# Mixture-of-experts rows: one gather per chunk by a list made with one-hot products, in place of a scatter into expert order

## The chip, the cores and the metric

One Trainium2 chip, one core. The metric is the device time of one launch in microseconds, as the median of several runs; the kernel before has 1685.17 us (three runs, 1684.55 to 1685.78). All data is float32.

## The reference

Two transformer-like blocks run one after the other on 512 tokens of width 1024. The last part of the second is a mixture of experts with 16 experts of hidden width 512; every token uses two of them. The change touches only this part and what prepares it:

```python
def hier_moe(x, w_group, b_group, w_expert, b_expert, w_gate, w_up, w_down):
    t = x.reshape(-1, D)                                   # 512 tokens x 1024
    pg = softmax(t @ w_group + b_group)                    # 4 groups
    gsel, pg_sel = argmax(pg), max(pg)
    e_logits = (t @ w_expert + b_expert).reshape(-1, 4, 4)[token, gsel]
    top_p, top_i = top_k(softmax(e_logits), 2)             # 2 experts of the group
    gates = one_hot(gsel * 4 + top_i, 16) * pg_sel * top_p / sum(top_p), summed over the 2
    y = 0
    for e in range(16):
        h = silu(t @ w_gate[e]) * (t @ w_up[e])
        y = y + gates[:, e:e + 1] * (h @ w_down[e])
    return y
```

`t` is the normalised residual; the output is `rms_norm(h + y) * final_norm`. Before this stand a state-space mixer, cross-attention, a convolutional feed-forward block, and a second pair of mixers with an output product (`w_out_2`).

## The kernel before, in words

Every engine has one instruction stream written by hand, in the order of the functions in `pe_program`, `act_program`, `dve_program`, `pool_program` and `sp_program`. Engines meet only through counting semaphores. Float32 products are made as three products: each operand is split into a high part (ScalarE copies it to the 32-bit "r" type, `w_hi`, `xh`, `hh`) and a low part (VectorE subtracts, `w_lo`, `xl`, `hl`), and TensorE adds hi·hi, hi·lo and lo·hi (L410 to L412 in the dense parts, L2810 to L2812 in the experts). SyncE queues the weight loads, 1 MB each.

**Output product** (`pe_w_out2`, L2342). Eight blocks of 128 features. After each one `pe_w_out2_turn` (L2326) makes the router logits of all tokens, as 20 rows by 512 columns (L2332, one float32 product per block, weights `wr`, added up over the blocks in bank 4), and turns the block into token rows with four transposes. ScalarE copies these to `xtm` (L2371) and sums their squares (L2373); VectorE scales them by the gain into `htm` (L2399).

**Routing** (`dve_route`, L2500). VectorE copies the logits out of PSUM, TensorE turns them back to token rows, VectorE scales and biases them per token tile (L2516, four instructions), and finds group and experts by small comparisons. `pre` holds running sums over the four token tiles (L2540). Two products, with a matrix of ones and a strictly triangular one, give each token's rank inside its experts and the count of each expert (L2459, L2460). From these VectorE builds `pick` (L2559), with which TensorE finds the token in each row of expert 0 (L2463), and writes this list to `first` (L2574). Then come `slot_of` (the row of each of a token's two copies in expert order, L2588) and `table` (which experts have more than 128 rows and need further chunks, L2600). Rows in expert order lie in chunks of 128, chunk e belonging to expert e; overflow chunks come after chunk 15.

**Moving the rows.** SyncE stores the normalised rows to DRAM, `scratch_rows` (L2738). GpSimd gathers chunk 0 from there by the list `first` (L2441, into `wrow`, also called `x_first`), and then scatters all rows, two copies of each, into `slot_rows` in DRAM with eight indirect transfers (L2446). When all eight have landed, SyncE loads chunk 1 and chunk 2 (`sp_rows`, L2713, called at L2741 and L2743) between two weight loads, and each later chunk once TensorE has turned the chunk two before it (L2752). `slot_rows` and eight chunks of `result_rows` are filled with zeros much earlier, in `pool_zero` (L2312), by 24 and 8 transfers of 512 KB.

**Experts** (`pe_experts`, L2816, with `act_experts`, `dve_experts`, `sp_experts`, `pool_experts`). A chunk has six weight parts of 1 MB: two of gate, two of up, two of down. Part n of chunk c is loaded when the low part of the same n of chunk c-1 is made. TensorE turns the rows ("x", eight transposes, L553), multiplies parts 0 to 3 (12 products each), turns the hidden rows ("h", four transposes), and multiplies parts 4 and 5. The orders are lists (`pe_order`, `act_order`, `dve_order`), and waits are counts in them. In steady state TensorE's order is w0 of c+1, h of c, w1 of c+1, x of c+2, w4 and w5 of c, w2 and w3 of c+1. Chunks 0 to 14 are written out. In the first, the order is x(0), w0, w1, x(1), w2, w3. On VectorE the low parts 2 to 5 of chunk 0 and the gates stand in `dve_route` (L2602), ahead of the rows of chunk 0 (L3004). A loop then runs chunk 15 and any overflow chunk (with this data the loop runs once); in each turn it also fetches the rows and weights of one further chunk, whether they are needed or not, and TensorE turns those rows (L2874) before the hidden rows of the turn. Results go to `result_rows` from GpSimd (L2772).

**End.** GpSimd gathers each token's two results by `slot_of` (L3059), and VectorE and ScalarE combine and normalise them.

## Time and profile before

| what | value |
|---|---|
| median of the runs | 1685.17 us |
| the profiled execution: its own time | 1681.13 us |
| its span, first to last instruction | 1680.0 us |
| TensorE busy / VectorE / ScalarE / GpSimd | 88% / 62% / 45% / 8% of the span |
| mean granted TensorE clock | 0.942 of full speed |
| DMA, mean over the span | 148 GB/s, 248.34 MB |
| the chain that ended last, by engine | TensorE 76%, VectorE 14%, ScalarE 5%, issue 2%, DMA 1%, GpSimd 1% |

Times are in us from the start of the span. In the trace the output product runs from about 1270 to 1318, routing until 1334, the chunks 0 to 14 until 1633, the loop turn until 1647, the end until 1680. A line of a timeline gives the start, the duration, the engine, the line of the kernel, the operation, output<-input with shapes, the number of merged instructions, and in brackets the idle time before it and what ended it. Matmuls are pipelined, so the distance of two starts says more than the duration.

### The profile page before, as it was taken

To read this page: it belongs to the slowest core of one execution; us is meant where nothing else is said; L and a number is where in the kernel's file an instruction comes from. 1 tells how busy PE (TensorE), PEld (TensorE's weight loads), DVE (VectorE), ACT (ScalarE), POOL (GpSimd) and SP (SyncE) were. 2 spreads that over 40 slices of the span, in tenths; PEclk is the share of its full clock that TensorE was granted. 3 is DMA by queue.
4 is the path that set the end of the run, shared out by engine and by line. 5 is a ranking of instruction groups with operands and counts; after the bars stand their busy time and mean duration, and the time that the engine had idled before them with its cause. 6 is when DMAs were issued, how large, how long until landed. Compare 5 with 4: busy or idle time off the path is not lost.

```text
span 1680.0 us, 17325 instructions
## 1 busy us (share of the span) xinstructions
PE 1485.0 (88%) x6792; PEld 1150.5 (68%) x6792; DVE 1039.4 (62%) x1342; ACT 756.8 (45%) x994; POOL 137.7 (8%) x162
## 2 busy tenths in 40 slices
PE   3889948979978999999999999999988499999981
PEld 1667618758756788788878778786545378888871
DVE  5849976465333555445554648845444668888876
ACT  4453315554333422122223443244445568878763
POOL 5400000000003100000000113200000200000002
PEclk8899869989999999999999999999999799999996
DMA  5121214212213922232212221110003599999984
GB/s 193 63 75 51 75 30 146 76 51 75 76 50 120 396 85 85 77 127 100 82 63 94 101 101 51 68 59 26 25 1 127 210 390 404 412 412 409 415 337 175
DMA packets 45953, 248.34 MB, mean 148 GB/s; under 512 B 6960, under 2 KB 8240, under 8 KB 23728
## 3 DMA queue, kind: packets, MB, share of 16 engines
q1 hardware_dynamic: 31488, 207.14, 32.3%
q0 software_dynamic: 9888, 36.18, 5.7%
q10 hardware_dynamic: 4496, 3.91, 0.7%
q8 instruction: 54, 0.88, 0.2%
q14 instruction: 27, 0.22, 0.0%
HBM read 213.66 MB, written 33.55 MB: 147 GB/s over the span
## 4 chain that ended last, share of the span: by engine, by line
PE 76%; DVE 14%; ACT 5%; issue 2%; DMA 1%; POOL 1%; ACTq 1%; DVEq 0%; POOLq 0%
PE bank L410 14%; PE bank L411 14%; PE bank L412 14%; PE bank L2810 5%; PE bank L2812 5%; PE bank L2811 5%; PE bank L553 3%; DVE w_lo L366 1%; PE bank L429 1%; PE bank L2133 1%; PE bank L2162 1%; DVE bu L832 1%; PE bank L430 1%; PE bank L431 1%; PE bank L469 1%
## 5 line engine op out<-in xcount | busy, mean ns | idle before, releaser
L410 PE MATMUL bank<-h_hi,w_hi 128*128 128x512 f32 x952 | 392.8, 413 | 28.8 <-DVE h_lo L490 19.6
L411 PE MATMUL bank<-h_lo,w_hi 128*128 128x512 f32 x952 | 381.8, 401 | 0.0
L412 PE MATMUL bank<-h_hi,w_lo 128*128 128x512 f32 x952 | 381.5, 401 | 0.0
L366 DVE TENSOR_TENSOR w_lo<-w_raw,w_hi 128x2048 fp32r<-128x2048 f32 (+3 forms) x89 | 197.5, 2219 | 91.6 <-ACT w_hi L360 90.9
L410 PEld LDWEIGHTS bank<-h_hi,w_hi 128*128 128x128 f32 x952 | 183.1, 192 | 86.9 <-DVE h_lo L490 20.6
L412 PEld LDWEIGHTS bank<-h_hi,w_lo 128*128 128x128 f32 x952 | 183.4, 193 | 43.1
L411 PEld LDWEIGHTS bank<-h_lo,w_hi 128*128 128x128 f32 x952 | 183.5, 193 | 40.8 <-issue 1.9
L360 ACT ACTIVATE w_hi<-w_raw 128x2048 fp32r<-128x2048 f32 (+3 forms) x89 | 158.4, 1780 | 59.9 <-PE bank L412 59.9
L2991 DVE TENSOR_TENSOR h_lo<-w_raw,h_hi 128x2048 fp32r<-128x2048 f32 x32 | 73.3, 2292 | 18.1 <-ACT h_hi L2893 18.1
L2991 DVE TENSOR_TENSOR lo_b<-raw_b,hi_b 128x2048 fp32r<-128x2048 f32 x32 | 73.2, 2288 | 14.2 <-ACT hi_b L2893 14.2
L410 PE MATMUL bank<-a_hi,w_hi 128*128 128x512 f32 x176 | 69.4, 395 | 4.5 <-DVE a_lo L1574 4.5
L411 PE MATMUL bank<-a_lo,w_hi 128*128 128x512 f32 x176 | 69.7, 396 | 0.0
L412 PE MATMUL bank<-a_hi,w_lo 128*128 128x512 f32 x176 | 69.1, 393 | 0.0
L1538 ACT ACTIVATE gc<-gc 128x512 f32<-128x512 f32 x22 | 13.9, 634 | 118.6 <-DVE gc L899 118.6
L2893 ACT ACTIVATE hi_b<-raw_b 128x2048 fp32r<-128x2048 f32 x32 | 61.1, 1911 | 10.1 <-PE bank L2812 10.1
L2893 ACT ACTIVATE h_hi<-w_raw 128x2048 fp32r<-128x2048 f32 x32 | 61.0, 1909 | 0.0
L2810 PE MATMUL bank<-h_hi,hh 128*128 128x512 f32 x128 | 53.0, 414 | 5.8 <-DVE hl L3015 4.4
L2810 PE MATMUL bank<-hi_b,xh 128*128 128x512 f32 x128 | 52.3, 409 | 6.3 <-DVE xl L3002 6.3
L1572 DVE TENSOR_TENSOR gc<-gc,bank 128x512 f32<-128x512 f32 x22 | 15.2, 689 | 61.9 <-PE bank L412 61.9
L2811 PE MATMUL bank<-h_hi,hl 128*128 128x512 f32 x128 | 51.6, 403 | 0.0
L2812 PE MATMUL bank<-h_lo,hh 128*128 128x512 f32 x128 | 51.4, 401 | 0.0
L2812 PE MATMUL bank<-lo_b,xh 128*128 128x512 f32 x128 | 50.7, 396 | 0.0
(556 smaller groups left out, 2817.0 us busy)
## 6 DMA issues: line engine op xcount, KB each, us to landing
w_raw<-in_params_dram SPq DMA_DIRECT2D x122, 1024.0 KB, 5.1
raw_b<-in_params_dram SPq DMA_DIRECT2D x51, 1024.0 KB, 7.9
slot_rows<-prm POOLq DMA_DIRECT2D x24, 512.0 KB, 19.4
w_raw<-in_params_dram SPq DMA_DIRECT2D x16, 704.0 KB, 4.0
xg<-slot_rows SPq DMA_DIRECT2D x16, 512.0 KB, 8.1
result_rows<-osb POOLq DMA_DIRECT2D x16, 512.0 KB, 8.1
result_rows<-prm POOLq DMA_DIRECT2D x8, 512.0 KB, 36.5
xt<-in_x_t_dram POOLq DMA_DIRECT2D x1, 2048.0 KB, 9.5
```

The source lines that it names most:

```text
L360: A.activation(k.w_hi[:, g % SPLIT, 0:size], k.raw[:, g % RAW, 0:size], ACT.Copy).then_inc(s.w_hi, 1)
L366: V.tensor_tensor(k.w_lo[:, g % SPLIT, 0:size], k.raw[:, g % RAW, 0:size], k.w_hi[:, g % SPLIT, 0:size].bitcast(F32), ALU.subtract).then_i ...
L410: PE.matmul(ps, wh, hi[:, c, 0:width], start=c == 0, stop=False)
L411: PE.matmul(ps, wh, lo[:, c, 0:width], start=False, stop=False)
L412: m = PE.matmul(ps, wl, hi[:, c, 0:width], start=False, stop=c == parts - 1)
L429: PE.matmul(ps, xh, wh, start=c == 0, stop=False)
L553: return k.nc.tensor.transpose(out, in_, k.ident[0:n, 0:n])
L2810: PE.matmul(o, xh[:, k0 + c, :], wh, start=first and c == 0, stop=False)
L2811: PE.matmul(o, xl[:, k0 + c, :], wh, start=False, stop=False)
L2812: m = PE.matmul(o, xh[:, k0 + c, :], wl, start=False, stop=final and c == 3)
L2893: done(A.activation(w_hi[n], raws[n], ACT.Copy), "w", n, c)
L2991: done(V.tensor_tensor(w_lo[n], raws[n], w_hi[n].bitcast(F32), ALU.subtract), "w", n, c)
```

## The change

The scatter, `slot_rows` and its 24 zero fills go away, and the eight fills of `result_rows` are spread out behind product blocks of the feed-forward part. VectorE makes, for all 16 chunks at once, the two factors of a one-hot product (`at_row`: which row of its chunk a token's copy takes, 128 columns; `tok_in`: the token's number in the column of its chunk), and eight products on TensorE give `tok`, the list of tokens of every chunk. GpSimd gathers each chunk from `scratch_rows` by a column of `tok`. What needs the overflow chunks (`slot_of`, `table`, the lists of chunks 16 to 23, the gates) moves out of the routing into the last written-out chunk: `dve_route_over` on VectorE, after the hidden rows of chunk 14, and `pe_tokens(k, 5, 0, OVER + 1)` on TensorE, before parts 4 and 5 of chunk 14. The router logits are made in token rows directly, four products of 20 columns per block. TensorE's first chunk becomes x(0), w0, w1, w2, w3, x(1), and on VectorE the rows of chunk 0 come before its low parts 4 and 5.

```diff
     k.g(G.memset(k.zero, 0.0))
     k.g.own()
-    rows, results = (x.rearrange("(n p) (u c) -> n p u c", p=P, u=2) for x in (k.slot_rows, k.result_rows))
+    results = k.result_rows.rearrange("(n p) (u c) -> n p u c", p=P, u=2)
     source = k.zero.rearrange("p (o c) -> p o c", o=1).broadcast_to([P, 2, T])
-    for n in range(SLOT_TILES):
-        G.dma_start(rows[n], source).then_inc(s.zeroed, 16)
     for n in range(E, SLOT_TILES):
+        G.wait_ge(s.gemm, BLOCK0["up0"] + 2 * (n - E))
         G.dma_start(results[n], source).then_inc(s.zeroed, 16)
...
         PE.wait_ge(s.mo_in, 1)
-    m = PE.matmul(k.bank[4][0:20, :], k.wr[:, b, :], k.xt[:, b, :], start=b == 0, stop=b == DB - 1)
+    for t in range(TT):
+        m = PE.matmul(k.bank[4][:, t * 20:t * 20 + 20], k.xt[:, b, t * P:t * P + P], k.wr[:, b, :], start=b + t == 0,
+                      stop=b == DB - 1 and t == TT - 1, skip_group_check=True)
     if b == DB - 1:
...
         A.wait_ge(s.mo_sq, b)
-    a(A.activation(k.xtm[:, :, b * P:b * P + P], turned(k, b), ACT.Copy))
+    if b < DB - 1:
+        act_w_out2_copy(k, b)
...
+def pool_rows(k, ids, i):
+    k.nc.gpsimd.indirect_dma_start(out=k.xg[:, i, :], out_offset=None, in_=k.dram["rows"][:, :],
+                                   in_offset=bass.IndirectOffsetOnAxis(ap=ids, axis=0)).then_inc(k.s.x_load1 if i else k.s.x_load0, 16)
...
     G.iota(k.tokid[:, :], [[P, TT]], base=0, channel_multiplier=1).then_inc(s.mo_iota, 1)
-    G.wait_ge(s.zeroed, ZEROED)
+    G.wait_ge(s.row_stored, 16 * TT)
     G.wait_ge(s.mo_slot, 1)
-    G.wait_ge(s.row_stored, 16 * TT)
-    G.indirect_dma_start(out=k.x_first[:, :], out_offset=None, in_=k.dram["rows"][:, :],
-                         in_offset=bass.IndirectOffsetOnAxis(ap=k.first[:, 0:1], axis=0)).then_inc(s.x_first, 16)
-    G.wait_ge(s.mo_slot, 2)
-    for t in range(TT):
-        for i in range(2):
-            G.indirect_dma_start(out=k.slot_rows[:, :], out_offset=bass.IndirectOffsetOnAxis(ap=k.slot_of[:, i, t:t + 1], axis=0),
-                                 in_=k.htm[:, t, :], in_offset=None).then_inc(s.scattered, 16)
+    for c in range(2):
+        pool_rows(k, k.tok[:, c:c + 1], c)
...
+def pe_tokens(k, ins, buffer, columns):
+    for i in range(2):
+        k.nc.tensor.wait_ge(k.s.mo_in, ins + i)
+        for t in range(TT):
+            m = k.nc.tensor.matmul(k.bank[7][:, 0:columns], k.at_row[buffer][:, i, t, :], k.tok_in[buffer][:, i, t, 0:columns],
+                                   start=i + t == 0, stop=i + t == TT)
+    m.then_inc(k.s.mo_cnt, 1)
 def pe_route(k):
...
-    for t in range(TT):
-        m = pe_turn(k, k.bank[7][:, t * 20:t * 20 + 20], k.lgs[:, t * P:t * P + P])
-    m.then_inc(s.mo_lgt, 1)
     PE.wait_ge(s.mo_htm, DB)
+    PE.wait_ge(s.mo_row, 1)
     PE.wait_ge(s.mo_in, 2)
     counts = k.bank[HBANK][:, 0:(TT + 1) * E]
-    PE.matmul(counts, k.ones[:, :], k.pre[:, :, :].rearrange("p t e -> p (t e)"), start=True, stop=False)
-    PE.matmul(counts[:, 0:TT * E], k.stri[:, :], k.r16[:, 0, :, :].rearrange("p t e -> p (t e)"), start=False, stop=True).then_inc(s.mo_cnt, 1)
-    PE.wait_ge(s.mo_in, 3)
+    PE.matmul(counts[:, 0:TT * E], k.stri_r, k.sel.rearrange("p t e -> p (t e)"), start=True, stop=False, skip_group_check=True)
     for t in range(TT):
-        m = PE.matmul(k.bank[7][:, 0:1], k.pick[:, t, :], k.tok_f[:, t:t + 1], start=t == 0, stop=t == TT - 1)
+        later = k.sel[:, t, :].rearrange("p (o e) -> p o e", o=1).broadcast_to([P, TT - t, E])
+        m = PE.matmul(counts[:, (t + 1) * E:].rearrange("p (n e) -> p n e", e=E), k.ones_r, later, start=False, stop=t == TT - 1,
+                      skip_group_check=True)
     m.then_inc(s.mo_cnt, 1)
+    pe_tokens(k, 3, 1, E)
 def act_route(k):
...
+def dve_at_row(k, buffer, row):
+    V, s = k.nc.vector, k.s
+    place = k.place.rearrange("p (o c) -> p o c", o=1).broadcast_to([P, TT, P])
+    for i in range(2):
+        at = row[:, i, :].rearrange("p (t o) -> p t o", o=1).broadcast_to([P, TT, P])
+        V.tensor_tensor(k.at_row[buffer][:, i, :, :], place, at, ALU.is_equal).then_inc(s.mo_in, 1)
...
-    V.wait_ge(s.zeroed, ZEROED)
-    V.wait_ge(s.mo_lgt, 1)
-    V.tensor_copy(k.lgs, k.bank[4][0:20, :]).then_inc(s.mo_lg, 1)
...
-        v(V.scalar_tensor_tensor(k.L[:, t, :], k.bank[7][:, t * 20:t * 20 + 20], rstd[:, t:t + 1], k.row[:, slice(*ROWS["router_b"])], ALU.mult, ALU.add))
+    V.wait_ge(s.mo_lgt, 1)
+    v(V.tensor_tensor(k.L[:, :, :], k.bank[4][:, 0:TT * 20].rearrange("p (t c) -> p t c", t=TT),
+                      rstd.rearrange("p (t o) -> p t o", o=1).broadcast_to([P, TT, 20]), ALU.mult))
+    v.own()
+    v(V.tensor_tensor(k.L[:, :, :], k.L[:, :, :], k.rows("router_b", TT, 20), ALU.add))
...
-        v.own()
-        x = V.tensor_tensor(k.pre[:, t + 1, :], k.pre[:, t, :], k.r16[:, 0, t, :], ALU.add)
-        if t == TT - 1:
-            x.then_inc(s.mo_in, 1)
-        else:
-            v(x)
+    V.tensor_tensor(k.sel.rearrange("p t (g j) -> p t g j", g=4), ohg4, wide(both), ALU.mult).then_inc(s.mo_in, 1)
     for i, oh in ((1, oh1), (2, oh2)):
         v(V.tensor_tensor(v16(i), ohg4, wide(oh), ALU.mult))
+    v.own()
+    pair = k.r16[:, 1:3, :, :]
+    for i in range(2):
+        v(V.tensor_tensor(k.tok_in[1][:, i, :, :], pair[:, i, :, :], k.tok_f[:, :].rearrange("p (t o) -> p t o", o=1).broadcast_to([P, TT, E]), ALU.mult))
     f = lambda x: x.rearrange("p t o -> p (t o)")
     v(V.tensor_tensor(e2, f(m2), f(m1), ALU.subtract))
     V.tensor_tensor(ex, gl, gm.broadcast_to([P, TT, 4]), ALU.subtract).then_inc(s.mo_dve, 1)
...
+    V.wait_ge(s.mo_cnt, 1)
+    mine = k.r16[:, 3:5, :, :]
+    rank = k.bank[HBANK][:, 0:TT * E].rearrange("p (o x) -> p o x", o=1).broadcast_to([P, 2, TT * E])
+    v(V.tensor_tensor(mine.rearrange("p i t e -> p i (t e)"), pair.rearrange("p i t e -> p i (t e)"), rank, ALU.mult))
+    v.own()
+    v(V.tensor_reduce(k.rk[:, 0, :, :].rearrange("p i (t o) -> p (i t) o", o=1), mine.rearrange("p i t e -> p (i t) e"), AX.X, ALU.add))
+    v.own()
+    dve_at_row(k, 1, k.rk[:, 0, :, :])
+    v(V.tensor_copy(k.ranks, k.bank[HBANK][:, 0:(TT + 1) * E]))
+    V.wait_ge(s.mo_cnt, 2)
+    V.tensor_copy(k.tok[:, 0:E], k.bank[7][:, 0:E]).then_inc(s.mo_slot, 1)
+    for n in (2, 3):
+        dve_expert_lo(k, k.dve_event, 0, n)
+    dve_expert_rows(k, 0)
+    for n in (4, 5):
+        dve_expert_lo(k, k.dve_event, 0, n)
+def dve_route_over(k):
+    V, s, v = k.nc.vector, k.s, k.v
     tiles, ends, base, delta, one = (k.cnt[:, i, :] for i in range(5))
+    rank = k.ranks[:, 0:TT * E].rearrange("p (t e) -> p t e", t=TT)
+    n_e = k.ranks[:, TT * E:]
     rows = lambda x: x.rearrange("p (o e) -> p o e", o=1).broadcast_to([P, TT, E])
-    V.wait_ge(s.mo_cnt, 1)
-    rank = k.bank[HBANK][:, 0:TT * E].rearrange("p (t e) -> p t e", t=TT)
-    n_e = k.bank[HBANK][:, TT * E:TT * E + E]
-    v(V.tensor_tensor(k.r16[:, 3, :, :], rank, rows(k.eoff[:, 0, :]), ALU.add))
-    v.own()
-    for t in range(TT):
-        x = V.tensor_scalar(k.pick[:, t, :], k.place[:, :], k.r16[:, 3, t, 0:1], k.r16[:, 0, t, 0:1], ALU.is_equal, ALU.mult)
-        if t == TT - 1:
-            x.then_inc(s.mo_in, 1)
-        else:
-            v(x)
     v(V.tensor_scalar(tiles, n_e, float(P), None, ALU.is_gt))
     for j in range(2, TT):
         v.own()
...
-    V.wait_ge(s.mo_cnt, 2)
-    V.tensor_copy(k.first[:, :], k.bank[7][:, 0:1]).then_inc(s.mo_slot, 1)
     v(V.scalar_tensor_tensor(delta, base, float(P), k.eoff[:, 1, :], ALU.mult, ALU.add))
...
-    v(V.tensor_reduce(slots, pair.rearrange("p i t e -> p (i t) e"), AX.X, ALU.add))
-    v.own()
...
+    rk, past, row, slot = (k.rk[:, i, :, :] for i in range(4))
+    v(V.tensor_reduce(slot.rearrange("p i (t o) -> p (i t) o", o=1), pair.rearrange("p i t e -> p (i t) e"), AX.X, ALU.add))
+    v.own()
+    V.tensor_copy(k.slot_of[:, :, :], slot).then_inc(s.mo_slot, 1)
...
+    v(V.tensor_scalar(past, rk, float(P), None, ALU.is_ge))
+    for j in range(2, TT):
+        v.own()
+        v(V.scalar_tensor_tensor(past, rk, float(P * j), past, ALU.is_ge, ALU.add))
+    v.own()
+    v(V.scalar_tensor_tensor(row, past, float(-P), rk, ALU.mult, ALU.add))
+    v.own()
+    v(V.tensor_tensor(slot, slot, row, ALU.subtract))
+    v.own()
     n = OVER + 1
+    for i in range(2):
+        tile = slot[:, i, :].rearrange("p (t o) -> p t o", o=1).broadcast_to([P, TT, n])
+        v(V.tensor_tensor(k.tok_in[0][:, i, :, 0:n], k.over[:, :].rearrange("p (o q) -> p o q", o=1).broadcast_to([P, TT, n]), tile, ALU.is_equal))
+    v.own()
+    for i in range(2):
+        token = k.tok_f[:, :].rearrange("p (t o) -> p t o", o=1).broadcast_to([P, TT, n])
+        v(V.tensor_tensor(k.tok_in[0][:, i, :, 0:n], k.tok_in[0][:, i, :, 0:n].bitcast(F32), token, ALU.mult))
+    v.own()
+    dve_at_row(k, 0, row)
...
-    for n in range(2, 6):
-        dve_expert_lo(k, k.dve_event, 0, n)
...
+    V.wait_ge(s.mo_cnt, 3)
+    V.tensor_copy(k.tok[:, E:], k.bank[7][:, 0:n]).then_inc(s.mo_slot, 1)
...
-    part(1, 2)
-    SP.wait_ge(s.scattered, 16 * 2 * TT)
-    sp_rows(k, 1, 1)
-    part(1, 3)
-    sp_rows(k, 2, 0)
+    for n in range(2, 6):
+        part(1, n)
     for n in (0, 1):
         part(2, n)
...
         if c + 2 < FIXED:
-            SP.wait_ge(s.m_pe, PE_AT["x", 1, c + 1])
-            sp_rows(k, c + 3, (c + 3) % 2)
...
-        SP.wait_ge(s.m_pe, q * len(PE_LOOP) + PE_BEFORE["x", 1])
-        sp_rows(k, q + E, LOOP_BUFFER)
...
 def pool_experts(k):
     G, s = k.nc.gpsimd, k.s
+    def rows(c):
+        G.wait_ge(s.m_pe, PE_AT["x", 1, c - 2])
+        pool_rows(k, k.tok[:, c:c + 1], c % 2)
+    rows(2)
+    rows(3)
     for c in range(FIXED):
+        if c + 4 < E:
+            rows(c + 4)
         G.wait_ge(s.m_act, ACT_AT["o", 1, c])
         pool_result(k, c, c % 2)
+    G.wait_ge(s.mo_table, 1)
...
+        G.wait_ge(s.m_pe, q * len(PE_LOOP) + PE_BEFORE["x", 1])
+        G.wait_ge(s.m_dve, q * len(DVE_LOOP) + (len(DVE_AT) + DVE_LOOP["i", 0]))
+        G.tensor_tensor(k.act_scrap[:, 1:2], k.ones[:, 0:1], k.ones[:, 0:1], ALU.add).then_inc(s.pool_step, 1)
+        pool_rows(k, k.tok_next[:, 0:1], LOOP_BUFFER)
+        G.wait_ge(s.pool_step, q + (k.g.n + 1))
         G.wait_ge(s.m_act, q * len(ACT_LOOP) + (len(ACT_AT) + ACT_LOOP["o", 1]))
         pool_result(k, q + FIXED, LOOP_BUFFER)
...
-        if c == 0:
-            PE.wait_ge(s.x_first, 16)
-        else:
-            PE.wait_ge(s.x_load1 if c % 2 else s.x_load0, 16 * ((c + 1) // 2))
+        PE.wait_ge(s.x_load1 if c % 2 else s.x_load0, 16 * (c // 2 + 1))
+        if c:
             PE.wait_ge(s.m_dve, DVE_AT["x", 1, c - 1])
         for half in range(2):
-            done(pe_turn_x(k, k.xg[:, c % 2] if c else k.x_first, half), "x", half, c)
+            done(pe_turn_x(k, k.xg[:, c % 2], half), "x", half, c)
...
-    PE.wait_ge(s.mo_slot, 1)
     rows(0)
     part(0, 0)
-    part(0, 1)
+    for n in range(1, 4):
+        part(0, n)
     rows(1)
-    part(0, 2)
-    part(0, 3)
...
             rows(c + 2)
+        else:
+            pe_tokens(k, 5, 0, OVER + 1)
         part(c, 4)
         part(c, 5)
         if c + 1 < FIXED:
...
+    act_expert_hi(k, done, 1, 2)
     rows(1)
-    act_expert_hi(k, done, 1, 2)
...
+    dve_expert_lo(k, done, 1, 0)
+    dve_expert_lo(k, done, 1, 1)
+    hidden(0)
+    dve_expert_rows(k, 1)
+    for c in range(FIXED):
+        if c:
+            hidden(c)
         dve_expert_lo(k, done, c + 1, 2)
         dve_expert_lo(k, done, c + 1, 3)
...
+        else:
+            dve_route_over(k)
         dve_expert_lo(k, done, c + 1, 4)
...
+        V.tensor_copy(k.tok_next[:, :], k.tok[:, bass.ds(q + E, 1)]).then_inc(s.m_dve, 1)
```

## Rows read from the trace of the kernel before

**Rows 1.** Busy time by window: from:to, length, PE, PEld, DVE, ACT, POOL, PEclk, DMA share, GB/s.

```profile
540.00:560.00 20.00, 20.00 (x84) 16.38 (x84) 11.62 (x14) 8.59 (x10) 12.50 (x18) 0.94 1.01 389
...
1400.00:1440.00 40.00, 40.00 (x190) 32.97 (x189) 36.15 (x23) 31.85 (x27) 1.06 (x2) 1.00 1.01 414
```

**Rows 2.** The chain in order of time around the routing: start, us, what.

```profile
1318.18 0.60 ACT xtm L2371
...
1346.55 5.22 DMA slot_rows<-htm,slot_of
1351.78 3.23 DMA xg<-slot_rows
```

**Rows 3.** GpSimd's timeline, 1295 to 1375.

```profile
1332.48 1.07 POOL L2441 DMA_INDIRECT wrow<-scratch_rows,first  x1 [61.53 <-DVE first L2574]
...
1335.16 1.96 POOL L2446 DMA_INDIRECT slot_rows<-htm,slot_of  x1 [0.30 <-issue]
...
1344.01 0.96 POOL L2446 DMA_INDIRECT slot_rows<-htm,slot_of  x1 [0.30 <-issue]
```

**Rows 4.** VectorE's timeline, 1300 to 1375.

```profile
1320.94 0.68 DVE L2516 SCALAR_TENSOR_TENSOR L<-bank,rt,row 128x20 f32<-128x20 f32 x4
...
1325.99 0.80 DVE L2540 TENSOR_TENSOR pre<-pre,r 128x16 f32<-128x16 f32 x4
...
1331.47 0.16 DVE L2574 CAST first<-bank 128x1 int32<-128x1 f32 x1 [1.09 <-PE bank L2463]
...
1333.98 2.28 DVE L2991 TENSOR_TENSOR w_lo<-raw_b,w_hi 128x2048 fp32r<-128x2048 f32 x1
...
1343.61 1.28 DVE L3002 TENSOR_TENSOR xl<-bank,xh 128x512 fp32r<-128x512 f32 x2
```

**Rows 5.** TensorE's timeline, 1300 to 1367.

```profile
1305.03 1.03 PE L2332 MATMUL bank<-xt,w_router 128*20 128x512 f32 x2
1305.99 0.66 PE L553 MATMUL bank<-ident,xt 128*128 128x128 f32 x4
...
1329.50 1.87 PE L2463 MATMUL bank<-tok_f,sqs 128*128 128x1 f32 x8 [1.47 <-DVE sqs L2559]
1336.80 1.94 PE L553 MATMUL bank<-ident,wrow 128*128 128x128 f32 x8 [5.43 <-DMA wrow<-scratch_rows,first]
1345.04 0.77 PE L2810 MATMUL bank<-hi_b,xh 128*128 128x512 f32 x1 [6.30 <-DVE xl L3002]
...
1351.77 0.39 PE L2812 MATMUL bank<-lo_b,xh 128*128 128x512 f32 x1
...
1362.94 0.40 PE L2810 MATMUL bank<-hi_b,xh 128*128 128x512 f32 x1
...
1365.70 0.60 PE L553 MATMUL bank<-ident,hid 128*128 128x128 f32 x4
```

**Rows 6.** Line L1728, small float32 products: ns min/median/max, first and last start.

```profile
L1728 PE MATMUL bank<-lf,ones x12: 256/256/256, 1009.1 to 1010.8; 128*128 128x8 f32 x12
...
L1728 PE MATMUL bank<-lf,tri x8: 170/256/256, 1009.0 to 1011.0; 128*128 128x8 f32 x8
```

**Rows 7.** TensorE's timeline, last written-out chunk and loop.

```profile
1614.45 0.66 PE L553 MATMUL bank<-ident,hid 128*128 128x128 f32 x4 [0.85 <-DVE hid L3011]
1619.50 0.77 PE L2810 MATMUL bank<-h_hi,hh 128*128 128x512 f32 x1 [4.39 <-DVE hl L3015]
...
1638.41 1.03 PE L553 MATMUL bank<-ident,xg 128*128 128x128 f32 x8
1639.35 0.66 PE L553 MATMUL bank<-ident,hid 128*128 128x128 f32 x4
```

**Rows 8.** VectorE's timeline, the same stretch.

```profile
1618.72 0.68 DVE L3015 TENSOR_TENSOR hl<-bank,hh 128x512 fp32r<-128x512 f32 x1
...
1630.08 2.29 DVE L2991 TENSOR_TENSOR h_lo<-w_raw,h_hi 128x2048 fp32r<-128x2048 f32 x1 [0.52 <-ACT h_hi L2893]
```

**Rows 9.** The page's DMA issues: KB each, median us to landing.

```profile
result_rows<-osb POOLq DMA_DIRECT2D x16, 512.0 KB, 8.1
```

86 lines of the change are left out of this document (44 added, 42 removed).

## The prediction

> **What bounds the kernel now.** I read the windows first, then the chain in order of time, then each engine's timeline at the places where TensorE stands still. In the expert stage the windows show TensorE busy for all of the 40 us at full clock, with the DMA engines busy all the time too, at 414 GB/s, and VectorE idle for under 4 us [rows 1]. A chunk takes 17.8 us: the hidden rows of chunk 0 are turned at 1365.70, those of chunk 14 at 1614.45, and (1614.45 - 1365.70)/14 = 17.8 [rows 5, 7]. The data is moved for about 7.3 MB a chunk (6 weight parts of 1.05, rows 0.52, result 0.52), which is 410 GB/s. TensorE sets the pace, with the DMA engines close behind. So the change can gain only where TensorE waits: between the end of the output product and about 1363, and at 1614 to 1619. The chain through the first stretch runs over VectorE's routing, GpSimd's issue of the scatter, its landing (5.22 us) and the load of chunk 1 (3.23 us) [rows 2]. TensorE's own timeline shows two waits there: 6.30 us for `xl` before the first product at 1345.04, and the turning of chunk 1 only at 1355.05. At the far end it waits 4.39 us for `hl` [rows 7].
>
> **Zero fills: 0.** The 24 removed fills saturate the DMA engines at 540 to 560, while TensorE is busy for all of the 20 us [rows 1]: the loads run three slots ahead and cover them. Gain 0, at most 1 us. GpSimd's eight remaining waits hold up nothing; it has no work there.
>
> **Logits: -0.6.** Before, a block's logits cost the distance from L2332 to the transposes, 1305.99 - 1305.03 = 0.96 us [rows 5]. After, they are four float32 products, two passes each. L1728's twenty passes with 8 columns start from 1009.0 to 1011.0, 2.0/19 = 0.11 apart [rows 6]. 8 x 0.11 = 0.88. Eight blocks: 8 x 0.08 = -0.6. Upper bound: the transposes' whole duration, 0.66/4 = 0.165 [rows 5], makes 1.3 a block, +2.9; lower bound: 0.94/8 = 0.12 is already what transposes of 128 columns are apart [rows 7], so nothing below -0.6 is expected. I take 0.11, since L1728 is the same kind of product at full clock.
>
> **List of tokens ready: -1.6.** Off the path to it: ScalarE's last copy to `xtm` (0.60, 0.5 between starts) [rows 2], half of L2516's 0.68 (four small instructions become two), and L2540's 0.80 (the running sums go into TensorE's products) [rows 4]: 0.5 + 0.3 + 0.8 = 1.6. The copy comes back ahead of the row scaling, where it fills the time it left. The rank products become five instead of two float32 ones; the list itself needs two 128-element steps (0.6), two 512-element comparisons (1.28, as L3002) and four closing products of 0.235 (L2463: 1.87 for 8 passes [rows 5]), 3.2 against 3.5 before. I call both level together. `first` was written at 1331.63 [rows 4]; the new list stands at 1330.0.
>
> **First rows: -5.6.** GpSimd starts the gather 0.85 later (1331.63 to 1332.48) and it arrived 4.3 after that (1332.48 to 1336.80) [rows 3, 5]: 1335.15. But VectorE now makes low parts 2 and 3 just then. Beside these subtractions an indirect issue took 1.96, and 0.96 once they were over [rows 3]; I add 0.9: 1336.0. The Trainium skill, "GPSIMD Engine Reference", section 1 Specifications, says that GpSimd shares its SBUF interfaces with VectorE and contends with its instructions that have two SBUF inputs; the trace agrees, and without that 0.9 the rows would come at 1335.1. Transposes (1.94), ScalarE's 0.6, VectorE's 0.68 and handovers of 0.2 make 3.4: the first product starts at 1339.4, against 1345.04. VectorE is free by then, 1330.0 + 2 x 2.2 = 1334.4, since parts 4 and 5 and the gates come later; before, they held `xl` back to 1343.61 [rows 4]. 5.6 us.
>
> **First chunk: -2.9.** From first product to first hidden turn it took 1365.70 - 1345.04 = 20.7, with the wait for the scatter inside. After: parts 0 and 1 as before, 7.0 (1351.77 + 0.23 - 1345.04), parts 2 and 3 at 2.76 (1362.94 to 1365.70 is one) = 5.5, the transposes of chunk 1 at full clock 0.94 (1638.41 to 1639.35 [rows 7]), then a new exposed handover, because x(1) now stands directly before w0 of chunk 1: 1.6 (0.6 + 0.68 + latencies; VectorE comes to it late, after a low part and the hidden rows), and 2.76. Sum 17.8, so -2.9. SyncE's queue loses the waits for scatter and rows; the weights of chunk 1 are there by about 1350, and part 4 is wanted after 1363. Together hidden(0) comes 8.5 earlier, 1357.2 against 1365.7, and the 0.6 of the logits besides.
>
> **Steady chunks: 0.** Gathers are issued 15 us before TensorE needs them; the bytes and the 4 KB row pieces are the same. That room of 15 us is the cover. VectorE's subtraction took 2.28 beside the scatter and 2.29 far from it [rows 4, 8], so it isn't slowed.
>
> **Overflow routing: +6.5.** It stands on VectorE after `hl` of chunk 14 (1618.72 + 0.6), and TensorE's `pe_tokens` waits for it with parts 4 and 5 queued behind. 21 instructions of 4 to 128 elements at 0.2 (L2540: 0.80 for four) are 4.3, two of 512 elements 1.3: 5.6. TensorE then closes four products at 0.235, plus 0.1. Part 4 starts at 1626.0 where it started at 1619.50 [rows 7, 8]. Nothing hides it: TensorE has no other work, and ScalarE, SyncE and the loop wait for part 4. The slow start of the products after a wait (half clock) is there in both. The rest of `dve_route_over` (2 us) ends before the next low part can be made, in 1634.
>
> **Rows of the loop: +0.3.** TensorE turns the next chunk's rows in the loop, at 1638.41 [rows 7], or 1644.9 after the 6.5. Before, they were loaded at 1615. Now GpSimd may issue only when VectorE has entered the loop, after the last low part: 1630.08 + 2.3 + 6.5 = 1638.9 [rows 8]. A handover (0.85), its small instruction (0.5) and 4.3 to 5.2 for the gather: 1644.6 to 1645.4. I take 0.3; if it lands after 8.1 us, as results do in this stage [rows 9], 3.4.
>
> **Sum:** -0.6 - 5.6 - 2.9 + 6.5 + 0.3 = -2.3 us (the -1.6 is in the -5.6). Against the profiled execution: 1681.13 - 2.3 = 1678.8. That execution was 4.0 below the median of 1685.17; I apply the difference to the median: 1682.9. About 0.2%, 3.4 us, is what a measurement of this kernel can tell from no change.
>
> **Rivals.**
> (a) The start gains more, -5. The first gather isn't slowed (lands 1335.1), and the clock, at half for seven products from 1345.04 (0.43 instead of 0.23), is up already because the wait ahead is 1.5 instead of 6.3 us: -0.9 - 1.4 = -4.6. For: the shorter wait. Against: TensorE has stood still 5 us before the transposes. 1680.3.
> (b) The loop's rows come late: +3.1 over the forecast, and 1.4 more if the clock falls: +0.8 to +2.2, 1686.0 to 1687.4. For: loads in this stage take 8.1 us. Against: few transfers are queued then.
> (c) The gather holds VectorE. Place: each steady chunk. `hl` is ready 0.8 us before TensorE needs it; if an issue of 1.9 us blocks VectorE there, TensorE loses 1.1 x 13 = 14 us: 1697. It decides from 0.8 us of blocking at that spot. For this, the Trainium skill, "SBUF — State Buffer", has a rule that the shared pair of ports is an exclusive lock, the second comer waiting for a whole instruction. Against: subtraction at 2.28 beside the scatter. This is the case slower than before.
> (d) The change doesn't do what it says: the gather of chunk 1, behind that of chunk 0 and four weight loads, comes as late as the scatter let it. It is needed at 1352 and issued by 1334: 18 us of room. Then the 2.9 are gone: +0.6, 1685.8.
>
> **Chances.** Forecast 0.53, (a) 0.25, (b) 0.13, (c) 0.05, (d) 0.04. The range reaches over (a), (b), (d) and the bounds of the logits: 1678.0 to 1687.5; (c) is left out. Faster by over 0.2% (below 1681.8): nearly all of (a), a fifth of the forecast, 0.35. Slower by over 0.2% (above 1688.5): (c) and the edge of (b), 0.08. Same: 0.57.
>
> **What would show it.** First product at 1339 less 0.6, hidden(0) at 1356.6, 17.8 us a chunk, a TensorE wait of about 10 us before part 4 of chunk 14, `xg` waited for in the loop by under 1 us. Wrong: a chunk over 18 us; a wait for `xg` at chunk 1; logits over 1.2 us a block.

## The result, and the profile after

The change makes the kernel slower: 1690.32 us (median of nine runs, 1687.73 to 1692.75) against 1684.04 (nine runs, 1681.51 to 1685.78), ratio 1.0037, interval 1.0029 to 1.0046, so +6.3 us where -2.3 was forecast. The profiled executions took 1690.61 and 1681.13. The bytes fell as announced: 231.57 MB moved (248.34 before), 16.78 MB written (33.55 before).

First the windows of the changed kernel (columns as in [rows 1]).

```profile
540.00:560.00 20.00, 20.00 (x87) 16.47 (x86) 11.39 (x13) 8.48 (x10) 0.00 (x0) 0.97 0.35 127
...
1284.00:1288.00 4.00, 2.21 (x11) 1.51 (x10) 2.99 (x3) 2.49 (x10) 0.00 (x0) 1.00 0.00 0
1288.00:1292.00 4.00, 4.00 (x18) 3.62 (x17) 1.10 (x2) 0.19 (x1) 0.00 (x0) 0.57 0.02 4
1292.00:1296.00 4.00, 4.00 (x12) 3.15 (x11) 0.69 (x1) 4.00 (x11) 0.00 (x0) 0.58 0.00 0
...
1338.00:1342.00 4.00, 0.00 (x0) 0.00 (x0) 0.02 (x1) 0.00 (x0) 0.85 (x1) 0.50 0.99 400
...
1400.00:1440.00 40.00, 40.00 (x194) 33.14 (x193) 36.15 (x24) 32.07 (x28) 4.58 (x4) 1.00 1.01 414
```

The same two windows of the kernel before, where [rows 1] has none:

```profile
1288.00:1292.00 4.00, 4.00 (x18) 2.68 (x18) 0.69 (x1) 2.99 (x10) 0.00 (x0) 1.00 0.00 0
1292.00:1296.00 4.00, 4.00 (x19) 2.87 (x18) 1.72 (x1) 3.76 (x11) 0.00 (x0) 1.00 0.02 4
```

Where the zeros were written the DMA share fell from 1.01 to 0.35 and TensorE is as busy as before [rows 1]; the expert stage is unchanged. Two things are new. From 1288 to 1296 the granted clock is near half (0.57 and 0.58, before 1.00), and products of 512 columns start 0.43 us apart (at 1292.43 and 1292.86), not 0.23. And at 1338 the DMA engines are full while TensorE stands still.

TensorE's timeline, the lines that answer to [rows 5] and, from 1612.98, to [rows 7].

```profile
1302.20 0.96 PE L2337 MATMUL bank<-w_router,xt 128*128 128x20 f32 x8
1303.01 0.64 PE L558 MATMUL bank<-ident,xt 128*128 128x128 f32 x4
...
1320.03 1.07 PE L2337 MATMUL bank<-w_router,xt 128*128 128x20 f32 x8 [0.78 <-DVE xt L2422]
...
1342.22 1.97 PE L558 MATMUL bank<-ident,xg 128*128 128x128 f32 x8 [8.81 <-DMA xg<-scratch_rows,tok]
1345.69 0.77 PE L2872 MATMUL bank<-hi_b,xh 128*128 128x512 f32 x1 [1.50 <-DVE xl L3060]
...
1358.73 1.03 PE L558 MATMUL bank<-ident,xg 128*128 128x128 f32 x8
1361.39 0.47 PE L2872 MATMUL bank<-hi_b,xh 128*128 128x512 f32 x1 [1.62 <-DVE xl L3060]
...
1364.22 0.60 PE L558 MATMUL bank<-ident,hid 128*128 128x128 f32 x4
...
1612.98 0.66 PE L558 MATMUL bank<-ident,hid 128*128 128x128 f32 x4 [0.85 <-DVE hid L3071]
1622.88 1.87 PE L2469 MATMUL bank<-xh,xl 128*128 128x8 f32 x8 [9.25 <-DVE xl L2529]
1624.61 0.77 PE L2872 MATMUL bank<-h_hi,hh 128*128 128x512 f32 x1
...
1647.06 1.97 PE L558 MATMUL bank<-ident,xg 128*128 128x128 f32 x8 [3.15 <-DMA xg<-scratch_rows,tok_next]
1648.82 1.06 PE L558 MATMUL bank<-ident,hid 128*128 128x128 f32 x4
1651.30 0.50 PE L2872 MATMUL bank<-h_hi,hh 128*128 128x512 f32 x1 [1.41 <-DVE hl L3115]
```

Three waits count: 8.81 us for chunk 0's rows, 9.25 for the one-hot rows of the overflow tokens, 3.15 for the loop's rows. Transposes that take 1.97 run at half clock, those of 1.03 at full.

GpSimd's timeline around the two gathers that came late (it answers to [rows 3]), and at its last small instruction.

```profile
1334.46 2.29 POOL L2448 DMA_INDIRECT xg<-scratch_rows,tok  x1 [61.71 <-DVE tok L2589]
1337.05 1.80 POOL L2448 DMA_INDIRECT xg<-scratch_rows,tok  x1 [0.30 <-issue]
...
1637.75 2.21 POOL L2841 TENSOR_TENSOR act_scrap<-ones 128x1 f32<-128x1 f32 x1 [3.46 <-DVE tok_next L3108]
1640.12 1.00 POOL L2448 DMA_INDIRECT xg<-scratch_rows,tok_next  x1 [0.16 <-POOL act_scrap L2841]
...
1662.96 0.18 POOL L3129 TENSOR_TENSOR act_scrap<-ones 128x1 f32<-128x1 f32 x1 [3.88 <-DMA result_rows<-osb]
```

VectorE's timeline at the same places (its cast answers to the one in [rows 4]):

```profile
1333.44 0.17 DVE L2589 CAST tok<-bank 128x16 int32<-128x16 f32 x1 [1.21 <-PE bank L2469]
1333.53 2.28 DVE L3053 TENSOR_TENSOR w_lo<-raw_b,w_hi 128x2048 fp32r<-128x2048 f32 x1
...
1637.62 2.29 DVE L3102 TENSOR_TENSOR lo_b<-raw_b,hi_b 128x2048 fp32r<-128x2048 f32 x1
```

SyncE's DMA queue at the same places.

```profile
1335.84 0.33 SPq L2772 DMA_DIRECT2D raw_b<-in_params_dram  x1
1338.04 12.25 SPq L2772 DMA_DIRECT2D w_raw<-in_params_dram  x3
...
1626.26 1.91 SPq L2772 DMA_DIRECT2D raw_b<-in_params_dram  x3
1628.41 9.68 SPq L2772 DMA_DIRECT2D w_raw<-in_params_dram  x3
```

The first gather is issued at 1334.46 and its rows are there at 1342.22, 7.8 us later; a weight load of 1 MB starts 1.4 us behind its issue, since VectorE's subtraction frees the buffer at about 1335.8. The loop's gather takes 6.9 us (1640.12 to 1647.06) beside six loads that begin at 1626.26. One GpSimd instruction of 128x1 elements takes 2.21 us beside VectorE's subtraction and 0.18 alone.

**By stages.** All the profiled executions can be cut at the same events of TensorE: the start of the output product, the last block's logits, chunk 0's rows, the first expert product, the hidden turns of chunks 0 and 14, part 4 of chunk 14, the loop's transposes of rows, part 4 in the loop, the end. Each number is the distance between two such starts. "Median" is the median less that of the kernel before in the same runs. The start of the output product itself lay anywhere from 1267.28 to 1272.75, with the same instructions of TensorE ahead of it, so it is left out.

| kernel | to logits | rows | product | hidden 0 | hidden 14 | part 4 | loop rows | loop part 4 | end | sum less before | median |
|---|---|---|---|---|---|---|---|---|---|---|---|
| before | 49.24 | 20.28 | 8.24 | 20.66 | 248.75 | 5.05 | 18.91 | 3.01 | 38.58 | 0 | 0 |
| after | 50.96 | 22.19 | 3.47 | 18.53 | 248.76 | 11.63 | 22.45 | 4.24 | 38.10 | +7.6 | +6.3 |
| e1 | 50.86 | 22.13 | 3.47 | 18.53 | 248.75 | 5.05 | 22.97 | 4.23 | 40.84 | +4.1 | +2.4 |
| e2 | 50.84 | 22.13 | 3.48 | 18.48 | 248.75 | 11.64 | 19.00 | 3.01 | 38.45 | +3.1 | +2.9 |
| e3 | 50.78 | 19.88 | 3.47 | 18.01 | 248.78 | 11.63 | 22.22 | 4.23 | 37.69 | +4.0 | +4.6 |
| e4 | 50.97 | 20.24 | 8.24 | 18.98 | 248.76 | 5.05 | 19.12 | 3.01 | 38.53 | +0.2 | -0.1 |
| e5 | 50.95 | 19.84 | 3.47 | 18.01 | 248.76 | 5.05 | 19.78 | 5.47 | 39.72 | -1.7 | -1.6 |
| e6 | 47.68 | 22.05 | 3.47 | 18.46 | 248.75 | 11.64 | 22.47 | 4.23 | 38.43 | +4.5 | +2.1 |
| e7 | 49.26 | 22.52 | 3.48 | 19.18 | 248.75 | 11.64 | 22.45 | 3.74 | 39.56 | +7.9 | +7.7 |
| e8 | 50.75 | 18.61 | 3.47 | 18.58 | 248.75 | 11.64 | 23.12 | 4.23 | 40.76 | +7.2 | +4.0 |
| e9 | 47.67 | 18.92 | 3.48 | 19.23 | 248.77 | 5.05 | 18.54 | 3.01 | 38.52 | -9.5 | -9.4 |
| e10 | 50.87 | 22.26 | 3.56 | 19.36 | 248.77 | 5.05 | 19.25 | 2.93 | 38.24 | -2.4 | -3.8 |
| e12 | 50.79 | 22.11 | 3.47 | 18.53 | 248.75 | 11.65 | 22.44 | 4.23 | 37.69 | +6.9 | +6.0 |

Most stages that an edit leaves alone come out within some 0.3 us again. The exceptions are the last, which has two sizes (below), e8's loop rows (23.12), e7's loop part 4 (3.74) and the stage to hidden 0. That one holds the products behind the wait for chunk 0's rows, and how many of them start at half clock (0.43 us apart, not 0.23) differs from kernel to kernel: 7 in the kernel before, in e3 and in e5, 9 to 11 in the others, 13 in e7. In e4, where nothing behind the routing was edited, it is 1.7 us shorter than in the kernel before. There is one trace of each kernel. Sum and median part by up to 3 us; the verdicts on single stages rest on the stages, those on the time on the ratios.

### The profile page after: what moved, and what is told of

Read it like the earlier page. It is cut to its first block, busy times and chain, and to the rows that moved or that the text cites. A ratio compares the mean times of both kernels' runs of the same rounds, so it can differ in the third digit from the quotient of the medians.

```text
span 1689.4 us, 17412 instructions
## 1 busy us (share of the span) xinstructions
PE 1491.5 (88%) x6845; PEld 1165.4 (69%) x6845; DVE 1042.8 (62%) x1353; ACT 755.9 (45%) x994; POOL 138.2 (8%) x147
## 2 busy tenths in 40 slices
DMA packets 41345, 231.57 MB, mean 137 GB/s; under 512 B 6448, under 2 KB 7728, under 8 KB 19120
## 3 DMA queue, kind: packets, MB, share of 16 engines
HBM read 213.66 MB, written 16.78 MB: 136 GB/s over the span
## 4 chain that ended last, share of the span: by engine, by line
PE 74%; DVE 15%; ACT 5%; issue 4%; DMA 1%; ACTq 1%; POOL 0%; POOLq 0%; DVEq 0%
PE bank L415 14%; PE bank L416 14%; PE bank L417 13%; PE bank L2872 5%; PE bank L2874 5%; PE bank L2873 5%; PE bank L558 3%; DVE w_lo L371 2%; PE bank L434 1%; PE bank L2138 1%; PE bank L2167 1%; DVE bu L837 1%; PE bank L436 1%; PE bank L435 1%; PE bank L474 1%
```

## The experiments

### Tokens of the overflow tiles late (e1)

```diff
-        else:
-            pe_tokens(k, 5, 0, OVER + 1)
         part(c, 4)
         part(c, 5)
+        if c + 1 == FIXED:
+            pe_tokens(k, 5, 0, OVER + 1)
```

> The changed kernel (1690.3 us, ratio 1.0037 to the kernel before) with one edit: the eight token products of the overflow tiles are issued behind parts 4 and 5 of chunk 14, not ahead of them. Main theory: in the changed kernel TensorE stands 9.25 us in front of these products for the one-hot rows of VectorE, and part 4 behind them runs most of its products at 0.43 us, not 0.23. With the edit the time falls by 6 to 8 us, to 1682.5 to 1684.5 (ratio 0.999 to 1.000), and the trace shows part 4 of chunk 14 about 5 us behind the hidden turns, waiting for hl as in [rows 7]. Rival: VectorE's overflow chain only moves its cost, since the tokens of the loop's gather then come later and the loop's rows (3.15 us late already) come later still; then the gain is 0 to 3 us and the idle time in front of the loop's transposes grows past 6 us.

Measured: 1686.01 us, ratio 1.0017 (1.0006 to 1.0028), where the changed kernel has 1.0037: about half of the gain expected (3.4 us by the ratios, where 6 to 8 were). TensorE's timeline of this kernel:

```profile
1616.66 0.76 PE L2872 MATMUL bank<-h_hi,hh 128*128 128x512 f32 x1 [4.39 <-DVE hl L3083]
...
1639.63 1.97 PE L558 MATMUL bank<-ident,xg 128*128 128x128 f32 x8 [3.00 <-DMA xg<-scratch_rows,tok_next]
...
1643.86 0.79 PE L2872 MATMUL bank<-h_hi,hh 128*128 128x512 f32 x1 [1.41 <-DVE hl L3115]
```

The 6.6 us are all back at part 4, and the wait is that of before, 4.39 for `hl`. The loop's rows are waited for 3.00 us all the same, now 9.0 us after their issue began (1630.66), because the six weight loads of the loop are still under way (DMA share 1.02 from 1632 to 1640). And the last stage takes 2.7 us more: its first product took 0.79, half clock, where the changed kernel's took 0.50. Theory right on the stall; two losses behind it were not in the sum.

### The loop's rows gathered early (e2)

```diff
+        if c == FIXED - 2:
+            G.wait_ge(s.mo_slot, 3)
+            G.wait_ge(s.m_pe, PE_AT["x", 1, E - 1])
+            pool_rows(k, k.tok[:, E:E + 1], LOOP_BUFFER)
...
-        G.wait_ge(s.m_pe, q * len(PE_LOOP) + PE_BEFORE["x", 1])
+        G.wait_ge(s.m_pe, q * len(PE_LOOP) + (len(PE_AT) + PE_LOOP["x", 1]))
...
-        V.tensor_copy(k.tok_next[:, :], k.tok[:, bass.ds(q + E, 1)]).then_inc(s.m_dve, 1)
+        V.tensor_copy(k.tok_next[:, :], k.tok[:, bass.ds(q + E + 1, 1)]).then_inc(s.m_dve, 1)
```

> The changed kernel with one edit: the rows of the first loop tile are gathered ahead of the loop, as soon as the overflow tokens are written, and each turn of the loop gathers those of the next. Main theory: the loop's gather is issued too late (1637.7, landing 1647.0, while the product ahead of the loop's transposes ends at 1643.9), which costs 3.15 us of waiting and about 1.2 us of products at half clock behind it. The time falls by 4 to 5 us (1685.3 to 1686.3, ratio 1.0007 to 1.0015); the idle time before the loop's transposes on the rows is gone. Rival: the loop's loss is the slow clock left by the stall in front of the token products; then the wait goes but the products still run slow, and the gain is under 2 us.

Measured: 1686.54 us, ratio 1.0020 (1.0011 to 1.0029), 3 us less than the changed kernel's; the two stages give back 3.45 + 1.23 = 4.7. TensorE's timeline in its loop:

```profile
1645.04 1.03 PE L558 MATMUL bank<-ident,xg 128*128 128x128 f32 x8
```

No wait stands at the transposes and they take 1.03, full clock, though the stall ahead of the token products is still there. The loss belongs to the late rows, and the rival falls.

### Weight loads behind the first gather (e3)

```diff
+    SP.wait_ge(s.x_load0, 16)
     for n in range(2, 6):
         part(1, n)
```

> The changed kernel with one edit: SyncE starts the weight parts 2 to 5 of chunk 1 only when the rows of chunk 0 have landed. Theory contention: the first gather landed 7.8 us after its issue began (4.3 forecast) because four weight parts of 1 MB and the second gather shared the DMA engines at 377 to 426 GB/s; behind the edit the rows land about 4.5 to 5.5 us after the issue began and the time falls by 2.5 to 3.5 us (ratio 1.0017 to 1.0022). Theory issue: the 2.29 us that GpSimd takes for the issue beside VectorE's 2.2 us subtraction, and the 1.80 of the second, are most of it; then the rows land at most 1 us earlier and the time falls by 0 to 1 us. The edit leaves both issues where they were. Third way: the weight parts themselves come late and a part of chunk 1 waits for them; then the time rises.

Measured: 1688.23 us, ratio 1.0034 (1.0021 to 1.0046) against 1.0037: the 2.5 to 3.5 us expected are not there, and by the time alone there is no verdict. The stages tell more. TensorE's timeline, the transposes of chunk 0's rows:

```profile
1339.77 1.97 PE L558 MATMUL bank<-ident,xg 128*128 128x128 f32 x8 [6.52 <-DMA xg<-scratch_rows,tok]
```

The gather was issued at 1334.30 with the same 2.29 and 1.80 us on GpSimd, and landed 5.5 us later, not 7.8. The stage to chunk 0's rows loses 2.3. So 2.3 of the 7.8 is contention with the loads; the rest is not. The stage to hidden 0 is 0.5 shorter too, since 7 products start at half clock, not 10. That is not shown to come from the loads: e8, below, keeps them away from the gather as well and has 10 and 18.58.

### VectorE's order: chunk 0's rows first (e8)

```diff
-    for n in (2, 3):
-        dve_expert_lo(k, k.dve_event, 0, n)
     dve_expert_rows(k, 0)
-    for n in (4, 5):
+    for n in range(2, 6):
         dve_expert_lo(k, k.dve_event, 0, n)
```

> The changed kernel with VectorE's order changed: the rows of chunk 0 ahead of the subtractions of weight parts 2 to 5 of chunk 0, so VectorE is idle while GpSimd issues the first gathers, and the weight parts 2 to 5 of chunk 1, which wait for those subtractions, start behind the gather. Theory lock: GpSimd's issue took 2.29 us because VectorE's 2.2 us subtraction ran beside it; here it takes about 1.0 us, and the rows land at least 1 us earlier than in the run with only the loads moved (5.5 us after the issue began, there): 4.0 to 4.5 us. Time 3.5 to 4.5 us below the changed kernel if no part of chunk 0 waits for its subtraction. Rival: 2.29 is what the first indirect issue costs, whatever VectorE does; then rows land after 5.5 us again.

Measured: 1688.19 us, ratio 1.0024 (1.0015 to 1.0034). GpSimd's timeline of this kernel:

```profile
1333.79 1.05 POOL L2448 DMA_INDIRECT xg<-scratch_rows,tok  x1 [61.52 <-DVE tok L2589]
1335.15 0.96 POOL L2448 DMA_INDIRECT xg<-scratch_rows,tok  x1 [0.30 <-issue]
```

and TensorE's:

```profile
1337.95 1.97 PE L558 MATMUL bank<-ident,xg 128*128 128x128 f32 x8 [5.22 <-DMA xg<-scratch_rows,tok]
```

With VectorE idle the two issues take 1.05 and 0.96, and the rows are there 4.2 us after the first began: 1.3 us better than in e3, as the theory said. The issue's length comes from VectorE's subtraction. The stage to the rows loses 3.6 us. Of that the ratio shows 2.2 (1.0024 against 1.0037), where 3.5 to 4.5 were expected; in the trace the last stage came out at its longer size, 40.76.

### The logits: new in the kernel before (e4), old in the changed one (e7), and the wait filled (e6)

```diff
-    m = PE.matmul(k.bank[4][0:20, :], k.wr[:, b, :], k.xt[:, b, :], start=b == 0, stop=b == DB - 1)
+    for t in range(TT):
+        m = PE.matmul(k.bank[4][:, t * 20:t * 20 + 20], k.xt[:, b, t * P:t * P + P], k.wr[:, b, :], start=b + t == 0,
+                      stop=b == DB - 1 and t == TT - 1, skip_group_check=True)
```

e4 is the kernel before with this edit (and without the copy and the transposes behind it), e7 the changed kernel with its reverse. e6 is the changed kernel with

```diff
+    for i in range(2):
+        PE.matmul(k.bank[7][:, :], k.xt[:, 0, 0:P], k.xt[:, 1, :], start=True, stop=True)
     for b in range(4, DB):
```

> The kernel before with one part of the change: the router's logits computed token by token (four products of 20 columns in each of eight blocks) in place of one 512 column product a block and four transposes behind, and no copy of the logits. Theory A: the clock fell in the changed kernel at 1288 us because the shorter products of TensorE keep it less busy next to a wait for the split weights; then this kernel shows the fall too, the logits' 2.2 us of gain are lost to it, and the time stands at -1 to +2 us of the kernel before (ratio 0.9994 to 1.0012). Theory B: the fall is of the clock's phase, has nothing to do with the logits, and this kernel gains 3 to 4.5 us: 2.2 in the eight blocks and 1.5 of the list (ratio 0.9973 to 0.9982).

> The changed kernel with work added: two fp32 products of 128x512, whose results nobody reads, on TensorE in the wait for w_lo at 1285.6 to 1287.4. Theory clock: the granted clock fell to 1.2 GHz at 1288 us because the new logits leave TensorE less to do ahead of this wait; with the wait filled the clock stays at 2.4 GHz from 1284 to 1300, the last logits' products start 3 to 3.5 us earlier against the start of the output product, and the time falls by 3 us (ratio 1.0018 to 1.0022). Rival: the fall comes from elsewhere; then the clock falls all the same and the time is unchanged or up to 1.8 us longer.

> The changed kernel with the logits taken back to the kernel before: one 512 column product a block, the copy of the logits, four transposes. The run with the new logits in the kernel before took 1.7 us longer from the output product to the last logits than the kernel before and started the list no sooner after them. Theory: the part is worth +1.7 us in the changed kernel as well, so the time falls by 1 to 2 us (ratio 1.0025 to 1.0031) and the granted clock is full from 1284 to 1300. Rival: behind the logits the changed kernel does gain from having no transposes (8.86 us from last logits to counts against 10.42); then 1.5 us come back there and the time is unchanged.

Measured: e4 1683.52 us, ratio 1.0001 (0.9990 to 1.0012); e6 1686.27, 1.0018 (1.0009 to 1.0027); e7 1691.86, 1.0041 (1.0028 to 1.0055). The windows (columns as above), e4 first:

```profile
1288.00:1292.00 4.00, 4.00 (x18) 3.69 (x17) 1.18 (x2) 0.14 (x1) 0.00 (x0) 0.58 0.02 4
1292.00:1296.00 4.00, 4.00 (x12) 3.09 (x11) 0.69 (x1) 4.00 (x11) 0.00 (x0) 0.57 0.00 0
```

then e6:

```profile
1284.00:1288.00 4.00, 3.92 (x17) 2.30 (x15) 3.87 (x4) 1.27 (x9) 0.00 (x0) 1.00 0.00 0
1288.00:1292.00 4.00, 4.00 (x26) 3.49 (x25) 0.69 (x1) 2.89 (x10) 0.00 (x0) 1.00 0.02 4
1292.00:1296.00 4.00, 4.00 (x24) 3.45 (x24) 1.62 (x1) 3.86 (x11) 0.00 (x0) 1.00 0.00 0
```

then e7:

```profile
1288.00:1292.00 4.00, 3.35 (x14) 1.92 (x15) 2.39 (x4) 0.10 (x1) 0.00 (x0) 1.00 0.00 0
1292.00:1296.00 4.00, 4.00 (x19) 2.44 (x18) 0.69 (x1) 4.00 (x11) 0.00 (x0) 1.00 0.02 4
```

The fall goes with the new logits into the kernel before and out of the changed one, and it is gone when the 1.8 us wait ahead of it is filled with products that nobody reads. (The new logits both give TensorE less to do and make this wait longer, 1.79 us after 1.52; which of the two decides was not separated.) The stage to the logits is 49.24 and 49.26 with the old ones, 50.75 to 50.97 with the new, 47.68 and 47.67 (e9) with the new and the filler. So the new logits cost 1.7 us as they stand and would gain 1.6. Theory A holds for the clock. The cost of 1.7 stands in the stage; in the time of a whole kernel neither run shows it. e4's time is the kernel before's, with an interval that reaches to +2.0 us. Its trace has the 1.7 at the logits and loses 1.7 again in chunk 0, most of it because the transposes of chunk 1's rows run at full clock there and at half in the kernel before. TensorE's timelines, e4 first, then the kernel before:

```profile
1358.36 1.09 PE L553 MATMUL bank<-ident,xg 128*128 128x128 f32 x8 [1.77 <-DMA xg<-slot_rows]
```

```profile
1355.05 1.97 PE L553 MATMUL bank<-ident,xg 128*128 128x128 f32 x8 [2.90 <-DMA xg<-slot_rows]
```

e7's time did not fall, a miss: its stage gave back the 1.7, but the three stages to hidden 0 took 1.0 more than in the changed kernel (0.6 of it three more products at half clock) and the last one 1.5. What a time does show is the filler: 3.2 us between e6 and the changed kernel, with intervals that do not meet.

### Three repairs (e5)

The edits of e2 and e3, and the token products between parts 4 and 5.

> The changed kernel with three edits: the token products between parts 4 and 5 of chunk 14 (by then their one-hot rows are there), the first loop tile's rows gathered ahead of the loop, and the weight parts 2 to 5 of chunk 1 started behind the landing of chunk 0's rows. Theory (the losses are three separate stalls, and they add): by the stages of the single traces the first repair is worth 6.6 us up to part 4, the second 4.7, the third 2.8, so the time is 1676 to 1679 (ratio 0.995 to 0.997), below the kernel before. Rival: with the stall gone the clock falls elsewhere in the tail, as it did in the run with the tokens behind part 5 (part 4 of the loop at half clock, 2.7 us longer to the end), and the weights of the loop crowd out the gather; then 1680 to 1683.

Measured: 1682.60 us, ratio 0.9988 (0.9978 to 0.9997). 8 us came back, not 11 to 14. That is the time of the rival, and half of its mechanism: part 4 of the loop does begin at half clock, but the gather is not waited for. All three stalls are gone, but TensorE's timeline has two others in the loop, for VectorE:

```profile
1640.64 0.66 PE L558 MATMUL bank<-ident,hid 128*128 128x128 f32 x4 [1.00 <-DVE hid L3118]
1644.08 0.80 PE L2878 MATMUL bank<-h_hi,hh 128*128 128x512 f32 x1 [2.78 <-DVE hl L3121]
```

VectorE's subtractions in the loop need its weights, and SyncE may load those only once `table` is written, at the end of the overflow routing: the first load began at 1627.37. That pointed to the table.

### Overflow routing undone (e10)

```diff
     for n in (2, 3):
         dve_expert_lo(k, k.dve_event, 0, n)
+    dve_route_over(k)
     dve_expert_rows(k, 0)
...
+    pe_tokens(k, 5, 1, OVER + 1)
     rows(1)
...
-        else:
-            dve_route_over(k)
```

> The changed kernel with one part of the change undone: the overflow routing of VectorE runs ahead of chunk 0's rows, as near as can be to where the kernel before had it, and its token products behind part 3 of chunk 0; nothing else. Theory: the move into chunk 14 alone costs more than the whole change lost. Part 4 of chunk 14 starts 5 us behind the hidden turns, not 11.6 (6.6 us), SyncE's loads of the loop start about 10 us earlier and so leave the loop's gather the DMA engines (3 to 4.8 us), against 1.4 us for chunk 0's rows late and 0.9 for the token products: 1680.5 to 1683.5 us (ratio 0.998 to 0.9998). Rival: the loop's gather is late because it is issued in the loop, whenever the weights start; then the loop keeps its 3 us of waiting and the time is 1684 to 1686.

Measured: 1680.28 us, ratio 0.9979 (0.9969 to 0.9989), just below what was expected: with this single part undone, the change gains. SyncE's queue in this kernel:

```profile
1618.21 4.16 SPq L2778 DMA_DIRECT2D raw_b<-in_params_dram  x3
```

GpSimd's timeline, the loop's gather:

```profile
1637.48 1.00 POOL L2448 DMA_INDIRECT xg<-scratch_rows,tok_next  x1 [0.16 <-POOL act_scrap L2847]
```

TensorE's timeline, part 4 of chunk 14 and the loop's transposes:

```profile
1622.58 0.77 PE L2878 MATMUL bank<-h_hi,hh 128*128 128x512 f32 x1 [4.40 <-DVE hl L3089]
...
1641.83 1.09 PE L558 MATMUL bank<-ident,xg 128*128 128x128 f32 x8 [0.62 <-DMA xg<-scratch_rows,tok_next]
```

The loads begin 4.4 us ahead of part 4, not 1.65 behind it. The loop's gather is issued where it was, 14.9 us behind part 4 (15.5 in the changed kernel), yet lands after 4.35 us, not 6.9: the wait shrinks from 3.15 to 0.62. The rival falls. VectorE's routing delayed chunk 0's first product by only 0.1 us, not 1.4; it fits into the wait for the gather. The token products cost 0.8 in chunk 0 (19.36 after 18.53), as expected.

### Everything together (e9)

e10's move, e8's order, e2's gather (in chunk 13) and e6's filler.

> The changed kernel with five edits: VectorE's overflow routing moved back from chunk 14 to the wait for the first gather, and its token products behind part 3 of chunk 0; chunk 0's rows ahead of the subtractions of its parts 2 to 5 on VectorE; the first loop tile's rows gathered in chunk 13; and the wait for w_lo filled with two idle products. Theory (the losses add): 6.6 us for the stall in chunk 14, 4.7 for the loop's rows, 3.3 for the clock fall, about 4 for the first gather, less 1 us for the token products and up to 1 us for the rows of chunk 0 late on VectorE; that is 16 to 17 us below the changed kernel, 1673 to 1676 us (ratio 0.994 to 0.996). With the table early, SyncE's loads of the loop start about 10 us earlier than in the run with three repairs (1616 instead of 1627), so hid and hl of the loop do not wait (there 1.0 and 2.8 us). Rival: the tail is bound by the clock and by its 6 MB of weights whatever comes first; then it stays above 1678.

Measured: 1674.75 us, ratio 0.9945 (0.9930 to 0.9961), faster than both kernels, where it was expected. TensorE's timeline, part 4 of chunk 14 and the loop:

```profile
1613.13 0.77 PE L2884 MATMUL bank<-h_hi,hh 128*128 128x512 f32 x1 [4.40 <-DVE hl L3095]
...
1631.67 1.03 PE L558 MATMUL bank<-ident,xg 128*128 128x128 f32 x8
```

In the loop no wait is left for rows or for `hid`.

### Zero fills back (e12)

```diff
-    for n in range(E, SLOT_TILES):
-        G.wait_ge(s.gemm, BLOCK0["up0"] + 2 * (n - E))
+    for n in range(SLOT_TILES):
+        G.dma_start(results[SLOT_TILES + n], source).then_inc(s.zeroed, 16)
+    for n in range(E, SLOT_TILES):
         G.dma_start(results[n], source).then_inc(s.zeroed, 16)
```

> The changed kernel with 24 more zero fills of 512 KB, issued without pause as in the kernel before, into a part of the results' memory that nobody reads. Theory: the zeros of the kernel before lay beside TensorE's work and cost nothing, so their removal gained nothing; the time is that of the changed kernel within 1 us (ratio 1.003 to 1.0045). Rival: they delayed weight loads or moved the clock; then the time is 2 us or more longer.

Measured: 1690.10 us, ratio 1.0037 (1.0023 to 1.0052), the changed kernel's own. At 540 to 560 the DMA share is 1.01 again and TensorE busy for all of the 20 us. 12.6 MB of zeros cost nothing that these runs can tell; the interval leaves room for about 2 us.

## Why the prediction was wrong, point by point

The forecast was no change to slightly faster, 1682.9 us, with a range up to 1687.5; the measured 1690.32 lies 2.8 us above that end, in "slower by over 0.2%", which had a chance of 0.08. The step that failed is the flight of two gathers: the prediction gave each about the time that the kernel before needed for one (4.3, at most 5.2 us), and did not see that SyncE's weight loads move with the steps that release them. They took 7.8 and 6.9 us. A second term had the wrong sign, the logits, for the clock.

- **Zero fills, 0.** Right as far as e12 can tell.
- **Logits, -0.6.** The cost of a block was even lower than forecast (1303.01 - 1302.20 = 0.81, forecast 0.88, before 0.96), and under the lower bound that the prediction named. What failed is that the step priced products and not what less work on TensorE beside a wait does to its clock. In the stage it is +1.7 (e4, e7), without the fall -1.6 (e6).
- **List ready, -1.6.** Right: from the last logits to GpSimd's issue 14.43 us (1320.03 to 1334.46) after 15.96 (1316.52 to 1332.48 [rows 3]), -1.5.
- **First rows, -5.6.** Measured 25.66 from last logits to first product after 28.52, -2.9. The list and the 3.4 from landing to product (3.47) hold. The term that failed is the flight of the gather: 5.2 were given it (4.3 and 0.9 for VectorE's neighbourhood), it took 7.8. The prediction saw that the subtractions move ahead and slow the issue, but not that SyncE's loads wait for them and so move too, into the gather: 2.3 (e3). VectorE's share is 1.3 (e8 against e3), where 0.9 stood.
- **First chunk, -2.9.** Measured -2.1 (18.53 after 20.66). The exposed handover is 1.62, as forecast. What failed is "parts 0 and 1 as before, 7.0": ten of their products start at half clock, not seven, 0.6 us. Why, no run shows. The 2.1 is not firm either: with the old order of the first chunk, e4 has 18.98, not 20.66.
- **Steady chunks, 0.** Right: 14 chunks take 248.75 to 248.78 us in every kernel here. The room of a gather is 34 us, not 15.
- **Overflow routing, +6.5.** +6.6. e10 gives it back whole. (21 instructions at 0.2 are 4.2, not 4.3; VectorE took 4.3 for them.)
- **Rows of the loop, +0.3.** This is the largest miss: +3.5 to the rows and +1.2 of half clock behind them. VectorE enters the loop 12.9 us behind part 4 (1637.52 - 1624.61), as worked out. But GpSimd's small instruction took 2.21, not 0.5, and the gather 6.9, not 4.3 to 5.2. "Against: few transfers are queued then" was the wrong sentence: the overflow routing also writes `table`, on which SyncE's six loads wait, so they moved behind it, from 1.3 us behind the hidden turns of chunk 14 (1615.76) to 13.3 (1626.26). The prediction followed the waits of TensorE and GpSimd behind the routing and left out SyncE's.
- **Rivals.** (b) happened, nearly at its price (3.1 over the forecast's 0.3 and 1.4, measured 3.5 and 1.2), with a chance of only 0.13; its time, at most 1687.4, was passed because the first gather and the logits failed as well. (a) asked for an unslowed gather and a kept clock; neither was there (and its -4.6 would make 1680.6, not 1680.3). (d) did not happen: chunk 1's rows are not waited for at 1358.73. (c) did not: VectorE's subtraction is 2.29 in the steady chunks. The Trainium skill, "SBUF — State Buffer", section "SBUF: two separate sides", has the rule that the second comer waits for the whole instruction of the first. With GpSimd second the trace agrees: its 128x1 instruction began 0.13 behind VectorE's subtraction and ended at 1639.96, 0.05 after it. With VectorE second it does not. In the kernel before, VectorE's subtraction began at 1333.98 [rows 4], 0.13 behind an issue on GpSimd, and took the usual 2.28; no gap stands before it. GpSimd's timeline of the kernel before:

```profile
1333.85 1.00 POOL L2446 DMA_INDIRECT slot_rows<-htm,slot_of  x1 [0.30 <-issue]
```


With the measured terms, each from one trace: +1.7 logits, -2.9 first rows, -2.1 first chunk, +6.6, +3.5 and +1.2, -0.5 in the last stage: +7.5 (+7.6 unrounded, as in the table), and the medians say +6.3.

## What to carry to other kernels

When a step is moved, list everything it signals, and for each queue that waits on it write down the new time of its transfers and what else flies then; here two groups of loads moved with it and hit two gathers. Put a gather's issue ahead of its need by what it takes beside full DMA engines (7 to 10 us here), not by what it takes alone (4.2). And when work is taken from TensorE next to one of its waits, look whether the clock holds; a chain of small instructions that nobody waits for soon belongs into a wait that exists (chunk 0's), not at the end.

## What the runs showed of the hardware

- The issue of the first gather on GpSimd took 2.28 to 2.29 us beside VectorE's 128x2048 subtraction and 1.05 with VectorE idle; a 128x1 tensor_tensor 2.17 to 2.22 and 0.18. The Trainium skill, "GPSIMD Engine Reference", section 1 Specifications, has GpSimd contend with VectorE's instructions of two SBUF inputs; these numbers agree.
- The gather of 128 rows of 4 KB was there 4.2 to 4.5 us after its issue began with the DMA engines free of loads, 5.5 with GpSimd slowed, 6.6 to 9.0 beside 1 MB loads. The median of the changed kernel's 16 gathers by the lists of chunks 0 to 15, most of them in the stage at 414 GB/s, is 9.9 us; in the steady chunks they are issued 34 us ahead of their need (1386.63, behind the transposes of chunk 3, for those of chunk 5 at 1421.10) and cost nothing.
- TensorE's granted clock fell to 1.2 GHz behind a wait of 1.8 us with two blocks of the logits' small products ahead of it; not behind one of 1.5 us with 512-column products in their place; and not with the wait filled. With the filler, whose results nobody reads, the stage is 3.3 us shorter.
- The last stage has two sizes, 37.7 to 38.6 or 39.6 to 40.8 us. The longer one stands in those kernels whose part 4 of the loop begins with a product of 0.79 to 0.80 (half clock). What decides between them was not tried.
